# First feed-forward by seven products of halves, modulation by scaled additions on VectorE behind up units

## What is computed

```python
def hybrid_layer(x, ...):
    ...
    x = x + rms_norm(mix, g_post_mix)
    h = rms_norm(x, g_pre_ffn)
    f = jnp.square(jax.nn.relu(h @ w_ff1)) @ w_ff2          # FFN1: 1024 -> 4096 -> 1024
    return x + rms_norm(f, g_post_ffn)

def second_block(x, c, ...):
    cond = jax.nn.silu(c)
    mod = jnp.einsum('bd,de->be', cond, w_ada[i]) + b_ada[i]   # 1024 -> 6 x 1024
    sh1, sc1, gt1, sh2, sc2, gt2 = jnp.split(mod, 6, axis=-1)
    h = _rmsnorm(x, g_mix[i]) * (1.0 + sc1[:, None, :]) + sh1[:, None, :]
    ...                                                     # attention (with rotary angles), convolution
    u = jnp.square(jax.nn.relu(jnp.einsum('bsd,df->bsf', h, w_up[i])))    # FFN2
    x = x + gt2[:, None, :] * jnp.einsum('bsf,fd->bsd', u, w_down[i])
    return _rmsnorm(x, g_final)
```

## Time and profile before

| what | us |
|---|---|
| median of 3 runs | 2704.44 (2695.72 to 2713.53) |
| the profiled execution's own time | 2707.75 |
| its span in the profile | 2705.9 |
| PE busy | 2585.9 |
| VectorE busy | 1539.8 |
| ScalarE busy | 979.8 |
| POOL busy | 421.6 |

### The profile page before, as it was taken

The page is one execution under the profiler, slowest core; times in us unless marked ns, Lnnn a source line. Parts: engine busy times, 40 slices in busy tenths (PEclk is TensorE's granted clock), DMA queues, the critical chain, the costliest instruction groups (busy, mean ns, idle before and its releaser), DMA issues.

```text
span 2705.9 us, 29849 instructions
## 1 busy us (share of the span) xinstructions
PE 2585.9 (96%) x11258; PEld 2058.4 (76%) x11258; DVE 1539.8 (57%) x2107; ACT 979.8 (36%) x1460; POOL 421.6 (16%) x393
## 2 busy tenths in 40 slices
PE   7999999989999999999998998899999999999985
PEld 5888677877888888888874786665778888888874
DVE  5242676365334243345657988775456666666655
ACT  4111466233112021122225586545334444334431
POOL 0000454002112121121000311110001111111111
PEclk9999799999999999999899999999999999999997
DMA  4111111233223222232310111000211111111111
GB/s 167 47 47 43 36 62 35 78 112 122 74 82 96 76 86 86 78 96 68 148 36 8 36 55 39 6 8 20 101 39 53 42 54 48 63 55 47 47 46 63
DMA packets 54355, 169.51 MB, mean 63 GB/s; under 512 B 7527, under 2 KB 11111, under 8 KB 54183
## 3 DMA queue, kind: packets, MB, share of 16 engines
q1 hardware_dynamic: 36496, 103.75, 12.0%
q0 software_dynamic: 17728, 63.98, 7.0%
HBM read 151.52 MB, written 12.68 MB: 61 GB/s over the span
## 4 chain that ended last, share of the span: by engine, by line
PE 83%; DVE 8%; ACT 4%; issue 4%; DMA 0%; SPq 0%; DVEq 0%; POOL 0%; ACTq 0%; POOLq 0%
PE G L1505 38%; PE G L2006 13%; PE TP L2025 11%; PE G L1525 4%; PE TP L1936 2%; ACT TK L1281 2%; PE G L1854 1%; PE G L1706 1%; PE TP L1727 1%; PE TP L1677 1%; PE G L1870 1%; PE TP L1548 1%; PE TP L1571 1%; ACT T L1267 1%; PE TP L1732 1%
## 5 line engine op out<-in xcount | busy, mean ns | idle before, releaser
L1505 PE MATMUL G<-XH,whi 128*128 128x512 f32 x1232 | 389.3, 397 | 1.9 <-ACT T L1267 1.1
L1505 PE MATMUL G<-XL,whi 128*128 128x512 f32 x1232 | 380.8, 390 | 0.0
L1505 PE MATMUL G<-XH,wlo 128*128 128x512 f32 x1232 | 380.4, 390 | 0.0
L962 ACT ACTIVATE whi<-raw 128x1024 fp32r<-128x1024 f32 x119 | 125.3, 1053 | 417.4 <-PE G L1505 378.4
L1505 PEld LDWEIGHTS G<-XH,wlo 128*128 128x128 f32 x1232 | 231.9, 188 | 49.0
L1505 PEld LDWEIGHTS G<-XL,whi 128*128 128x128 f32 x1232 | 231.8, 188 | 49.0
L1505 PEld LDWEIGHTS G<-XH,whi 128*128 128x128 f32 x1232 | 228.8, 189 | 52.7 <-issue 6.0
L2716 DVE SCALAR_TENSOR_TENSOR XT<-TP,mod,XT 128x512 f32<-128x512 f32 x224 | 167.8, 750 | 56.7 <-PE TP L2025 56.7
L2065 DVE TENSOR_TENSOR wlo<-raw,whi 128x1024 fp32r<-128x1024 f32 x107 | 130.9, 1224 | 114.1 <-ACT whi L962 113.8
L2025 PE MATMUL TP<-UOH,RH 128*128 128x512 f32 x448 | 175.3, 391 | 6.8 <-issue 6.8
L2025 PE MATMUL TP<-UOL,RH 128*128 128x512 f32 x448 | 175.0, 391 | 0.0
(11 more groups left out here) (340 smaller groups left out, 4708.6 us busy)
## 6 DMA issues: line engine op xcount, KB each, us to landing
raw<-slabs SPq DMA_DIRECT2D x183, 512.0 KB, 3.5
ADA<-ada POOLq DMA_DIRECT2D x48, 512.0 KB, 3.8
x_spill<-XT POOLq DMA_DIRECT2D x2, 4096.0 KB, 14.3
BIAS<-tab_spill POOLq DMA_DIRECT2D x8, 960.0 KB, 5.0
XT<-xT SPq DMA_DIRECT2D x8, 512.0 KB, 9.1
XRE<-xT POOLq DMA_DIRECT2D x8, 512.0 KB, 3.8
XRE<-x_spill POOLq DMA_DIRECT2D x8, 512.0 KB, 3.7
XT<-x_spill POOLq DMA_DIRECT2D x1, 4096.0 KB, 14.5
```

The lines of the kernel that those rows point to most:

```text
L962: act.activation(whi[b][:, :, :].rearrange("p k n -> p (k n)"), raw[b][:, :], ACT.Copy).then_inc(hi_ready, 1)
L1505: last = pe.matmul(G[b][:, half, :], w[b][:, k, :], x[:, k, half * HALF:(half + 1) * HALF], start=(at_k == 0 and n == 0), stop=(at_k == KT ...
```

## The change

FFN1 goes by the same units as FFN2: the functions take the feed-forward's number w (0 or 1) and are run twice. Tiles of FFN1 are evicted by VectorE as max(G, 0)·RBS, except the first three, which ScalarE evicts and VectorE scales once RBS is there. RING goes from 10 to 8, the sums of a pair's weights keep two places in place of four (two of the four sums are written over quarters of `raw`, the last of them after a unit that reads it), and POOL makes four operations of 256 columns for three.

The modulation leaves POOL. SP loads `w_ada` in 96 halves of 256 KB into two buffers. VectorE makes a sum by one scaling and seven scaled additions of 128x128, each waiting for the one before; four places of RED hold sums. PE makes the columns after the last unit of tiles 4k+1, 4k+2 and 4k+3 of parts k = 1 to 7: 1, 3 and 3 columns, at the last place 2. VectorE adds the bias part by part. The rotary angles go into the input product of the first layer, on 128x64, by way of memory; the first slab of IN2 is split four units ahead of FFN1's end.

```diff
-RING = 10
+RING = 8
...
+ADA_SUMS = {(k, j): n for k in range(1, FF_PARTS) for j, n in ((1, 1), (2, 3), (3, 2 if k == FF_PARTS - 1 else 3))}
...
+    ADA_STEPS = []
+    for part in range(1, FF_PARTS):
+        n = FF_TILES * part
+        steps = [UNIT_AT[(UP,) + unit] for unit in [(n + 1, v) for v in (1, 2, 3)] + [(n + 2, v) for v in range(4)] + [(n + 3, v) for v in range(3)]]
+        chunks = sum(ADA_SUMS[(part, j)] for j in (1, 2, 3))
+        ADA_STEPS += [steps[h * len(steps) // (2 * chunks)] for h in range(2 * chunks)]
...
+        def ada_load(h):
+
+            a, b = divmod(h, 2)
+            if h < 2:
+                sp.wait_ge(op_lo, LOWS_OF_PART)
+            else:
+                sp.wait_ge(red_made, KT_N // 2 * (h - 1))
+            sp.dma_start(ADA[:, b, :, :].rearrange("p k n -> p (k n)"), ada[a, :, HALF * b:HALF * (b + 1)]).then_inc(ada_loaded[b], 16)
...
+            pool.tensor_tensor(out[:, 0, :], quarter[:, 2, :], quarter[:, 3, :], ALU.subtract).then_inc(sums_made, 1)
+            pool.wait_ge(sums_made, made + 1)
+            pool.tensor_tensor(quarter[:, 2, :], quarter[:, 2, :], quarter[:, 0, :], ALU.subtract).then_inc(sums_made, 1)
+            pool.wait_ge(sums_made, made + 2)
+            pool.tensor_tensor(out[:, 1, :], quarter[:, 3, :], quarter[:, 2, :], ALU.subtract).then_inc(sums_made, 1)
+            pool.wait_ge(sums_made, made + 3)
+            pool.wait_ge(unit_lo, w * N_PREPARED + RING_AT[(PAIR, pair, 2)] + 1 - FIRST_PREPARED)
+            pool.tensor_tensor(quarter[:, 1, :], quarter[:, 1, :], out[:, 1, :], ALU.subtract).then_inc(sums_made, 1)
...
-        with pool.Fori(0, 22) as t:
-            for b in range(2):
-                pool.wait_ge(ada_loaded[b], t * 16 + 16)
-                pool.tensor_tensor(ADA[b][:, :, :], ADA[b][:, :, :],
-                                   silc[:, :].unsqueeze(2).broadcast_to([P, KT_N, P]), ALU.mult).then_inc(ada_prod, 1)
-                pool.wait_ge(ada_red, t * 2 + (1 + b))
-                ada_load(t * 2 + (2 + b), b)
...
+        for tab, rest in ((COS, 1.0), (SIN, 0.0)):
+            pool.memset(tab[:, :], rest).then_inc(rot_filled, 1)
+        pool.wait_ge(rot_filled, 2)
+        pool.wait_ge(rot_stored, 32)
+        for n, tab in enumerate((COS, SIN)):
+            for first in (0, ROT_ROWS, DH, DH + ROT_ROWS):
+                pool.dma_start(tab[first:first + ROT_ROWS, :], rot_spill[n]).then_inc(rot_loaded, 16)
...
+            elif n >= 2:
+                pe.wait_ge(unit_lo, w * N_PREPARED + r + 1 - FIRST_PREPARED)
+                if v == 0 and w == 0 and n - 2 >= SCALED_LATE:
+                    pe.wait_ge(scaled, n - 1)
...
+        def ada_sums(part, j):
+
+            pe.wait_ge(bank_read, EVICTED_BY[(FF_TILES * part - 1, 5)])
+            first = ADA_FIRST[(part, j)]
+            for a in range(first, first + ADA_SUMS[(part, j)]):
+                pe.wait_ge(red_made, KT_N * (a + 1))
+                pe.matmul(TP[1][:, 1, a:a + 1], RED[a % 4][:, :], ones[:, 0:1], start=True, stop=True,
+                          skip_group_check=True).then_inc(col_made, 1)
...
+            for kind, n, v in FF_UNITS:
+                if kind == PAIR:
+                    pair_unit(w, n, v)
+                    continue
+                up_unit(w, n, v)
...
+                if w == 0 and v == 3 and divmod(n, FF_TILES) in ADA_SUMS:
+                    ada_sums(*divmod(n, FF_TILES))
...
-                        dve.tensor_reduce(RED[a % 2][:, :], ADA[a % 2][:, :, :].rearrange("p k n -> p n k"), AX.X,
-                                          ALU.add).then_inc(ada_red, 1)
...
+            dve.wait_ge(unit_done, tile_done(n) + 1)
+            if n > SCALED_LATE:
+                dve.wait_ge(op_lo, 5 * ((n - 3) // 2 + 1))
+            dve.scalar_tensor_tensor(out=out, in0=Gf[(FFN1 + n) % 2], scalar=0.0, in1=RBS[:, :], op0=ALU.max,
+                                     op1=ALU.mult).then_inc(scaled, 1)
...
+        def ada_half(a, b):
+
+            dve.wait_ge(ada_loaded[b], 16 * (a + 1))
+            if a == 0 and b == 0:
+                dve.wait_ge(silc_ready, 1)
+            if a >= 4 and b == 0:
+                dve.wait_ge(col_made, a - 3)
+            for j in range(KT_N // 2):
+                k = KT_N // 2 * b + j
+                if k:
+                    dve.wait_ge(red_made, KT_N * a + k)
+                    dve.scalar_tensor_tensor(out=RED[a % 4][:, :], in0=ADA[:, b, j, :], scalar=silc[:, k:k + 1], in1=RED[a % 4][:, :],
+                                             op0=ALU.mult, op1=ALU.add).then_inc(red_made, 1)
+                else:
+                    dve.tensor_scalar(RED[a % 4][:, :], ADA[:, b, j, :], silc[:, 0:1], None, ALU.mult).then_inc(red_made, 1)
```

More of the change, by code:

```diff
@@ L267, in build @@
     ATTN = [KT[:, 1, :]] + [QT[:, k, :] for k in range(1, 4)]
[L269 to L275, removed]
+    RBS = at("RBS", [P, S], A_WLO)
+    ADA = at("ADA", [P, 2, KT_N // 2, P], A_WLO + 4096)
+    RED = [at(f"RED{b}", [P, P], A_R + 81920 + 512 * b) for b in range(4)]
+    assert A_R + 81920 + 2048 <= nc.sbuf_usable_end
     UOH = at("UOH", [P, PRODUCTS, 2, HALF], A_R, F32R)
@@ L847, in _ @@
+        pool.wait_ge(x_split, 24)
+        for pair in range(PAIRS):
+            weight_sums(0, pair)
         pool.wait_ge(spilled, 16)
@@ L1802, in _, with unit_parts, up_unit @@
-        ffn(FFN1, 0, 16)
+        def unit_parts(w, unit, xh, xl):
+            at_r = RING_AT[unit] % RING
+            return ((RH[w][:, at_r, :], xh), (RH[w][:, at_r, :], xl), (RL[:, at_r, :], xh))
+        def up_unit(w, n, v):
+            base = FF_BASE[w]
+            b, r = (base + n) % 2, RING_AT[(UP, n, v)]
+            if n < 2 and v == 0:
+                pe.wait_ge(lo_ready, base + n + 1)
+                pe.wait_ge(psum_free[b], (base + n) // 2 + 1)
+            elif n >= 2:
+                pe.wait_ge(unit_lo, w * N_PREPARED + r + 1 - FIRST_PREPARED)
+                if v == 0 and w == 0 and n - 2 >= SCALED_LATE:
+                    pe.wait_ge(scaled, n - 1)
+                elif v == 0:
+                    pe.wait_ge(relued, SCALED_LATE * w + n - 1)
+            for j in range(2):
+                k = 2 * v + j
+                if n == 0:
+                    pe.wait_ge(x_split, FF_SPLITS[w] + k + 1)
+                for at_n, (wt, x) in enumerate(unit_parts(w, (UP, n, v), XH, XL)):
+                    for half in range(2):
+                        last = pe.matmul(G[b][:, half, :], wt[:, j * P:(j + 1) * P], x[:, k, half * HALF:(half + 1) * HALF],
+                                         start=(k == 0 and at_n == 0), stop=(k == KT_N - 1 and at_n == 2))
+            last.then_inc(unit_done, 1)
@@ new lines, in tile_scaled @@
+        def tile_scaled(n):
+            out = tile(0, n)[:, :]
+            if n < SCALED_LATE:
+                dve.wait_ge(relued, n + 1)
+                dve.tensor_tensor(out, out, RBS[:, :], ALU.mult).then_inc(scaled, 1)
+                return
+            dve.wait_ge(unit_done, tile_done(n) + 1)
[3 more added lines that the diff above has]
+                                     op1=ALU.mult).then_inc(scaled, 1)
@@ L2396, in _ @@
         last.then_inc(mod_ready, 1)
-        norm(D, RMS_EPS, KT_N, SQF, SSQF, first=7, between=lambda: lo(IN2 + 1, (IN2 + 1) % 2), last_on_pe=True)
+        norm(D, RMS_EPS, KT_N, SQF, SSQF, first=6, between=lambda: lo(IN2 + 1, (IN2 + 1) % 2), last_on_pe=True)
         def add_even(k):
@@ L2751, in _ @@
[L2751 to L2762 removed]
+        ffn(1)
```

735 lines of the change are left out of this document (333 added, 402 removed).

## The result

The changed kernel takes 2776.07 us (median of 3, 2769.65 to 2790.05) for 2704.44 before: a ratio of 1.0277, 95% interval 1.0247 to 1.0306. It is slower, as forecast, by the mechanism forecast, but by 72 us where 37 were foretold, and 1 us outside the range.

The account below looks back on a forecast made before the run. PE's matmuls were taken to bound the kernel. 2707.75 − 45.7 (matmuls) + 6.0 (end) + 76 (modulation sums) = 2744.1 us, on the median's scale 2741; range 2702 to 2775 for 8 in 10.

Parts of the forecast that it names:

- the mechanism: First feed-forward's up units: VectorE's modulation sums come late and PE waits for them, +76 us in all.
- the price of an operation: Modulation sums on VectorE: 351 ns for each 128x128 operation, 2.8 us a sum, 135 us for all 48.
- the gain of the matmuls: First feed-forward: 192 fewer matmuls at .22667 us each; the term, with two added stalls, is −45.7 us.
- the end: End of the first feed-forward: variance starts 11.65 us after PE's end, as in the second, for 5.7 before: +6.0.
- (a): Rival: VectorE keeps up with the sums, so the matmul gain comes out, 2665 us; chance .13.
- (b): Rival: stall without late loads or POOL contention, 7.9 us a part, 2716; chance .29 including the ground up to the forecast.
- (d): Rival: pair units stall for want of two ring buffers, 5 us on either case; no chance of its own given.
- (c): Rival: every wait at its upper end, loads 4 us and operation gaps 1.7, 16 a part, 2773; chance .18.
- The stall of a part: First feed-forward's up units: sums 10.2 us late plus 1.3 for loads, 11.5 a part in six parts.
- The last part: Part 7 of the first feed-forward: one sum less and one pair unit later, so a stall of 7 us.
- The start: First part of the first feed-forward: its first four tiles catch up late behind the norm, estimated at 2 us.
- The two waits priced in the stretch: Up units, on VectorE: POOL's additions cost 2.3 us (1.6 to 3.2), late weight loads 1.3 (0 to 4) a part.

Follow-up runs that it names:

- e4: Changed kernel with 18 filler matmuls on PE ahead of the second wait for sums and 14 ahead of the third: a part 94.96 us for 96.25.
- e2: Changed kernel with two halves of the modulation's weights loaded once and used for all sums: a part 95.08 us for 96.25.
- e3: Changed kernel with POOL's first feed-forward weight sums on 8 of 256 columns from the third pair on: a part 92.02 us for 96.25.

## Why the prediction was right or wrong

Right: the direction and the mechanism, with the waits at the second and third place and none at the first; the price of an operation (351, measured 351 without POOL); the gain of the matmuls and the second feed-forward, unchanged; the end (var is taken up at 1370.3, some 12 us after PE's last product as in the earlier trace rows; foretold +6.0, S has 5.6). Of the rivals (a), (b) and (d) fell. (c), 2773, was nearest, and by luck: its loads of 4 were 1.5 in the rows, and it has no half clock.

That the third place came so near, 42.5 after T0 for 41.4, is luck in part. From the first sum to that place VectorE's old work is 11.8 us (35.0 less 20.8 of sums and 2.4 of tiles) for the 14.82 taken, not least because what POOL costs fell on the sums; its gaps are 4.0 for 1.3: the loads' 1.5, .7 for a high part, and 1.8 of small ones, which only (c) counted. The sums are 20.8 for 19.6.

Wrong: the size. From the third tile to the last product the sum gave 726.8 us; the trace has 757.1 (600.89 to 1354.99 + 3.01). Three terms of it were mis-sized:

- **The stall of a part**, 11.5, with the half clock behind the third place at nothing. Measured over five parts: 12.8 at the third place, and 1.4 of half clock behind it. The fall of the clock was in the earlier trace rows, and the signs at the end of the prediction name it, but neither the sum nor a rival has a price for it; at the second place the prediction says that it costs nothing more, where e4 and e2 show some .3 to 1 us. The six parts took 578.7 us (648.04 to 1226.72) for the 563.6 of the sum: 15 more, 2.5 of them in the first piece of the first part (36.51 for 34.00).
- **The last part**, 7. It took 91.5 us for the 77.5 of the second feed-forward, .8 of it columns: 13. One sum less at the last place takes nothing from the waits at the second place, and I had reckoned only with the third. Here they are 4.34 and 4.25 us, with 2.9 of half clock behind them (11.04 for 36):

```profile
1290.15 0.59 PE L1859 MATMUL TP<-cst,RED 128*128 128x1 f32 x2 [4.34 <-DVE RED L2429]
1294.99 0.59 PE L1859 MATMUL TP<-cst,RED 128*128 128x1 f32 x2 [4.25 <-DVE RED L2429]
```

- **The start**, 2. The chain's first rows:

```profile
599.27 1.23 DVE SSQ L2345
600.50 0.34 DVE RL L2350
600.89 10.06 PE G L1826 x36
```

From 600.89 to 648.04 are 47.2 us for 12 up units, a pair unit and the norm, 37.7: 9.4 lost, and the estimate of 2 was not worked out from rows. The tiles' chain (low part, scaling, square, operand, one engine waiting for the other) could have been added up from rows 10. Also, the third tile's weights are split behind the norm's additions on VectorE (the first two rows), 2.3 us later than before; that step of the order I had not looked at.

These are 15, 6 and 7 of the 30 us by which the product is over the sum, and the 2.3 ahead of it; S is 32 over the 36.3 foretold (68.5). The two waits priced in the stretch were about right: POOL 2.3, for the 2.6 of VectorE's busy time that e3 gives back, and the loads 1.3, for 1.5 in the rows and .8 in e2.

## What to carry over

Work that is hidden on average is late if it is due at a point: add up what stands in the queue ahead of that point, and compare it with the time to that point and not with the engine's free time in the stage. The remedy is to start such work in the stretch before, an operation at a time, and then to see to the loads; and a point can't be moved freely, since behind the next tile's operands it waits for them. Where PE waits for some us, price the half clock behind the wait as part of it, not as a risk, and ask which engine waits for the slow unit. And when an experiment shortens a wait, read the clock behind it before the gain is put down to what was taken out: of e3's 4.2 us 1.2 were PE's.

## What the runs showed of the hardware

VectorE's additions of 128x128 took .71 to .78 us beside POOL's for .36 alone. In a stretch in which VectorE was busy 35.0 of 39.0 us and POOL 5.6, POOL's additions cost VectorE 2.6.

PE's granted clock fell to .50 within the wait at the second place (1.00 from 902 to 904, .85 from 904 to 906, .50 from 906 to 908), and was at .50 again behind a wait of 3.0 us that came 13 us later; with matmuls filling that second wait (e4) it stayed at 1.00. The length of the wait at the third place does not tell by itself: behind 1.77 and 1.71 us the 36 matmuls took 9.77 and 9.84, behind 2.16 they took 8.29.
